# Order changes on VectorE and ScalarE in a two-layer hybrid attention trunk

## The reference

```python
for i in range(DEPTH):                       # DEPTH = 2
    x = x + 0.5 * swiglu(rmsnorm(x, ln_ffn1[i]), w_ffn1_gu[i], w_ffn1_down[i])
    h = rmsnorm(x, ln_mix[i])
    x = x + (even_mixer(h, ...) if i % 2 == 0 else odd_mixer(h, ...))
    x = x + 0.5 * swiglu(rmsnorm(x, ln_ffn2[i]), w_ffn2_gu[i], w_ffn2_down[i])
    gate = jax.nn.sigmoid(rmsnorm(x, ln_ple[i]) @ w_ple_gate[i])
    x = x + gate * (p[i] @ w_ple_proj[i])
return rmsnorm(x, ln_final)
# rmsnorm(x, g) = x * rsqrt(mean(x * x) + 1e-6) * g;  swiglu = (silu(x Wg) * (x Wu)) Wd
```

## Time and profile before

| | |
|---|---|
| median of 3 runs | 1047.08 us (1047.06 to 1048.47) |
| the profiled execution's own time | 1047.2 us |
| its span, first to last instruction | 1045.5 us |
| TensorE (PE) matmuls | busy 1030.4 us, 99% of the span, 6596 instructions |
| TensorE weight loads (PEld) | busy 921.8 us, 88% |
| VectorE (DVE) | busy 757.4 us, 72% |
| ScalarE (ACT) | busy 587.9 us, 56% |
| GpSimd (POOL) | busy 51.6 us, 5% |
| mean granted TensorE clock | 0.997 of full speed |
| device memory read | 183.59 MB, 177 GB/s over the span |
| chain that ended last | PE 94%, DVE 4%, issue 1%, ACT 1%, DMA 1% |

### The profile page before, as it was taken

How to read it: one execution, slowest core, us unless ns; L and a number is a source line. 1 busy time by engine, 2 the same in 40 slices (tenths; PEclk the granted TensorE clock), 3 DMA queues, 4 the chain that set the end, 5 groups by cost and what they waited for, 6 DMA issues and landing times.

```text
span 1045.5 us, 18268 instructions
## 1 busy us (share of the span) xinstructions
PE 1030.4 (99%) x6596; PEld 921.8 (88%) x6596; DVE 757.4 (72%) x1352; ACT 587.9 (56%) x1003; POOL 51.6 (5%) x100
## 2 busy tenths in 40 slices
PE   9999999999999999999999999999999999999996
PEld 8888888998888888888998888889987888888896
DVE  5988765667658887765888787656766787886576
ACT  6666545545646665554666565445654665654463
POOL 1000001000011000000010000010000200000000
PEclk9999999999999999999999999999999999999998
DMA  9675457594315655457647654577733376545741
GB/s 318 211 234 165 143 160 212 175 299 135 116 63 189 214 171 183 132 166 231 215 143 238 196 173 139 155 208 223 241 112 102 126 239 194 189 138 147 212 148 41
DMA packets 225384, 185.52 MB, mean 177 GB/s; under 512 B 3665, under 2 KB 223537, under 8 KB 225201
## 3 DMA queue, kind: packets, MB, share of 16 engines
q1 hardware_dynamic: 222832, 180.94, 55.5%
q10 hardware_dynamic: 2496, 3.86, 1.1%
HBM read 183.59 MB, written 1.07 MB: 177 GB/s over the span
## 4 chain that ended last, share of the span: by engine, by line
PE 94%; DVE 4%; issue 1%; ACT 1%; DMA 1%; DVEq 0%; SPq 0%; ACTq 0%
PE ps L1386 42%; PE ps L1391 22%; PE ps L1317 4%; PE ps L1308 4%; PE ps L1309 4%; PE ps L1310 4%; PE ps L1318 2%; PE ps L1501 2%; PE ps L1502 2%; PE ps L1503 2%; DVE wsp L895 1%; PE ps L1577 1%; PE ps L1590 1%; PE ps L1618 1%; DVE probs L1110 1%
## 5 line engine op out<-in xcount | busy, mean ns | idle before, releaser
L895 DVE TENSOR_TENSOR wsp<-raw,wsp 128x1024 fp32r<-128x1024 f32 (+1 forms) x381 | 416.3, 1109 | 59.9 <-ACT wsp L590 59.1
L590 ACT ACTIVATE wsp<-raw 128x1024 fp32r<-128x1024 f32 (+1 forms) x381 | 354.4, 957 | 25.5 <-PE ps L1310 20.6
L1386 PE MATMUL ps<-xsA,wsp 128*128 128x512 f32 x960 | 229.0, 391 | 0.0
L1386 PEld LDWEIGHTS ps<-xsA,wsp 128*128 128x128 f32 x960 | 176.4, 188 | 34.3
L1386 PE MATMUL ps<-hff,wsp 128*128 128x512 f32 x616 | 145.0, 390 | 0.0
L1386 PEld LDWEIGHTS ps<-hff,wsp 128*128 128x128 f32 x616 | 113.8, 188 | 22.8
L1391 PEld LDWEIGHTS ps<-xsA,wsp 128*128 128x128 f32 x960 | 122.9, 191 | 4.5
L1391 PE MATMUL ps<-xsA,wsp 128*128 128x256 f32 x960 | 124.7, 283 | 0.0
L910 DVE TENSOR_TENSOR sq<-ps,sq 128x512 f32<-128x512 f32 x88 | 60.5, 688 | 87.4 <-ACT sq L606 87.0
L606 ACT ACTIVATE sq<-ps 128x512 f32<-128x512 f32 x88 | 51.9, 590 | 110.7 <-PE ps L1391 109.0
L652 ACT ACTIVATE xsA<-xT,gains 128x256 fp32r<-128x256 f32 x48 | 24.4, 507 | 135.2 <-DVE xT L1044 120.4
(11 more groups left out here) (205 smaller groups left out, 1440.5 us busy)
## 6 DMA issues: line engine op xcount, KB each, us to landing
raw<-in_w_ffn_gu_dram SPq DMA_DIRECT2D x87, 1024.0 KB, 5.1
raw<-in_w_ffn_down_dram SPq DMA_DIRECT2D x64, 704.0 KB, 4.6
raw<-in_w_in_even_dram SPq DMA_DIRECT2D x11, 1024.0 KB, 6.2
raw<-in_w_in_odd_dram SPq DMA_DIRECT2D x9, 1024.0 KB, 6.1
raw<-in_w_ple_gate_dram SPq DMA_DIRECT2D x8, 1024.0 KB, 5.8
raw<-in_w_out_even_dram SPq DMA_DIRECT2D x4, 1024.0 KB, 5.1
raw<-in_w_out_odd_dram SPq DMA_DIRECT2D x4, 1024.0 KB, 7.0
raw<-in_w_ple_proj_dram SPq DMA_DIRECT2D x2, 1024.0 KB, 4.9
```

The source lines that it names most:

```text
L590: act.activation(wsp[:, s, 0, half * n:(half + 1) * n], raw[:, s, half * n:(half + 1) * n], ACT.Copy).then_inc(hi, 1)
L895: dve.tensor_tensor(wsp[:, s, 1, sl], raw[:, s, sl], wsp[:, s, 0, sl].bitcast(F32), ALU.subtract).then_inc(lo, 1)
L1386: pe.matmul(ps[:, bank, :], whi, moving.rearrange("p s t -> p (s t)"), start=first and i == 0, stop=False)
```

## The change

Four places are edited.

1. `mixer_in` on VectorE calls `inverse_root` with `ahead=2`: two units go between the diagonals and the wait for `row_done`.
2. In an even attention step of a softmax group, VectorE divides head i before the units, not behind them.
3. In the last token group, the squares of the last two column groups are summed by VectorE (`add_squares`: a product with a running sum, whose start is the sum so far) and no longer by ScalarE. The sum of the first two and the epsilon are folded in ahead (`squares_so_far`). The last inverse root is the square root from ScalarE's table, its reciprocal on VectorE and one Newton turn (`last_root`), in place of the bit trick and three turns. ScalarE loads the table for the square root behind its last sigmoid. The first token group is done as before.
4. In `first_tiles`, TensorE computes the second chunk in runs: eight high products of tile 2, eight of tile 3, each four of them behind their half's `hi`, and then the low products of both.

```diff
@@ ScalarE, ple_rows
-                    if i:
+                    if 1 <= i < 7:
                         squared(i - 1)
                     advance(ptr[0] + 2)
                     if i == 5:
                         scaled(0)
-                squared(len(GATE_ROWS) - 1)
+                nc.scalar.preload_act_table_set("sqrt_and_others")
+                act.wait_ge(var_ready, 1)
+                act.activation(rfin[:, 1:2], var[:, 1:2], ACT.Sqrt).then_inc(root_taken, 1)
                 scaled(1)
@@ VectorE, mixer_in
-                        inverse_root(norm)
+                        inverse_root(norm, ahead=2)
@@ VectorE, attention_step
                     logits(g + 1)
+                    normalise(g)
                     advance(units)
-                    normalise(g)
@@ VectorE, ple_rows
+                def squares_so_far():
+                    part = rtmp[:, 1:2]
+                    dve.wait_ge(row_squared, 6)
+                    step(dve.tensor_scalar(part, row_sq[:, 4:5], row_sq[:, 5:6], 1.0 / D_MODEL, ALU.add, ALU.mult))
+                    dve.tensor_scalar(part, part, EPS, None, ALU.add).then_inc(part_ready, 1)
+
+                def add_squares(i, start, total, done):
+                    dve.tensor_tensor_reduce(sq[:, i % 2], yT[:, i], yT[:, i], 1.0 / D_MODEL, start, ALU.mult, ALU.add, total).then_inc(done, 1)
+
+                def last_root():
+                    v, y, tmp, half = var[:, 1:2], rfin[:, 1:2], rtmp[:, 0:1], nhalf[:, 1:2]
+                    dve.wait_ge(var_ready, 1)
+                    dve.tensor_scalar(half, v, -0.5, None, ALU.mult).then_inc(nstep, 1)
+                    state["n"] += 1
+                    dve.wait_ge(root_taken, 1)
+                    step(dve.reciprocal(y, y))
+                    step(dve.tensor_scalar(tmp, y, y, half, ALU.mult, ALU.mult))
+                    dve.tensor_scalar(y, tmp, 1.5, y, ALU.add, ALU.mult).then_inc(rfin_ready, 1)
+                    dve.wait_ge(rfin_ready, 2)
@@ VectorE, ple_rows, in the loop over the row tiles
+                    if i == 6:
+                        squares_so_far()
+                        dve.wait_ge(part_ready, 1)
+                        dve.wait_ge(row_squared, 6)
+                        add_squares(6, rtmp[:, 1:2], rcol[:, 0:1], part_ready)
+                    if i == 7:
+                        dve.wait_ge(part_ready, 2)
+                        add_squares(7, rcol[:, 0:1], var[:, 1:2], var_ready)
                     advance(ptr[0] + 2)
...
-                final_root(1)
+                last_root()
@@ TensorE, first_tiles
-                for r in range(1, RING):
+                tiles = [[(chunk_w(1, k, n * P), xs[:, k]) for k in range(KD)] for n in range(2)]
+                for n in range(2):
+                    reuse(2 + n)
+                    for b in range(2):
+                        pe.wait_ge(hi, 3 + b)
+                        high_run(2 + n, tiles[n][4 * b:4 * b + 4], first=b == 0)
+                for n in range(2):
+                    for b in range(2):
+                        pe.wait_ge(lo, 3 + b)
+                        mm = low_run(2 + n, tiles[n][4 * b:4 * b + 4], last=b == 1)
+                    mm.then_inc(tile_done, 1)
+                for r in range(2, RING):
```

More of the change, by code:

```diff
@@ L293, in trunk @@
         row_squared, row_scaled, rfin_ready = sem("row_squared"), sem("row_scaled"), sem("rfin_ready")
+        part_ready, var_ready, root_taken = sem("part_ready"), sem("var_ready"), sem("root_taken")
         y_low, y_high, stored = sem("y_low"), sem("y_high"), sem("stored")
```

## The result

| | before | after |
|---|---|---|
| median, first comparison | 1047.07 us (4 runs, 1046.94 to 1048.47) | 1041.39 us (4 runs, 1041.16 to 1041.61) |
| ratio | | 0.9941, 95% interval 0.9928 to 0.9953 |
| median, second comparison | 1047.41 us (9 runs) | 1041.71 us (5 runs); 0.9943, 0.993 to 0.9957 |
| profiled execution, its span | 1047.2 us, 1045.5 us | 1041.61 us, 1039.9 us |
| VectorE, ScalarE busy | 757.4, 587.9 us | 757.4, 588.3 us |

What follows compares the result with a forecast made beforehand. TensorE's work, its few stops and the end were taken to bound the kernel. Terms 1.35 + 2.0 + 1.4 + 0.2 = 4.95 us off the profiled 1047.2 gave 1042.1 us against the median, range 1041.0 to 1044.2.

Steps and rivals of the forecast that it cites:

- What bounds the kernel: Whole kernel: PE is busy 99% of the span, so time is TensorE's work, its few stops and the end.
- Part 1: Mixer input, both layers: two units ahead remove TensorE's stops of 0.61 and 0.54 us before tile 4; gain 1.35 us.
- Part 2: Even softmax steps: dividing ahead of the unit removes five TensorE stops, 2.1 us, less 0.15 at the long stop; 2.0 us.
- the long stop: Layer 1, 790.25 us, head 10: VectorE is full, so the stop moves to head 12's transposes; -0.15 us.
- Part 3: Kernel end, last `yT` to first scaling: shorter squares and root, table load hidden behind the last sigmoid; gain 1.4 us.
- the two unseen operations: Kernel end: running-sum product taken as 0.48 us and ScalarE's root as 0.22, both from nearest rows.
- Part 4: Second chunk at the start: computing in runs takes 5.57 us instead of 5.79; gain 0.2 us, bounds 0 and 0.25.
- A: Kernel end: the table switch isn't hidden, Part 3 gives 0.35 us, total 1043.2 us; chance 10%.
- B: Softmax steps: Part 2 is given back everywhere and gives 0, total 1044.1 us; chance 10%.
- C: Layer 1: the long stop shortens for good, head 12's logits coming earlier, 0.94 + 0.15 more, 1041.0 us; chance 7%.
- D: Seven softmax steps: units arrive late, TensorE stops 1.1 us in each, total 1051.9 us, slower; chance 3%.
- E: All parts: the change does less than it says, half swallowed by other waits, total 1044.6 us; chance 7%.

Runs made afterwards that it cites:

- e7: The changed kernel with ScalarE's square-root table loaded only once the variance is ready, behind a one-column copy: 1043.28 us, 1.57 more than the changed kernel.
- e6: The changed kernel with layer 1's mixer output taking its two VectorE units behind the division of head 12: 1040.70 us, against 1041.71 for the changed kernel.
- e11: The kernel before, unchanged, profiled again to find where slow runs lose time: 1048.62 us.
- e15: The kernel before plus an unused load of the square-root table on ScalarE after the last squares: ratio 0.9997 to the kernel before.
- e16: The kernel before with three semaphores declared and used by nothing: ratio 1.0003 to the kernel before.
- e1: The kernel before with only two units put ahead in the row wait of both mixers: 1045.86 us, ratio 0.9986.

## Where the prediction held, and which steps failed

**What bounds the kernel** held: the time is TensorE's work, its stops and the tail, and stops read from starts, not brackets, gave each of parts 1 to 3 to 0.15 us.

**Part 1**, 1.35 forecast, 1.40 measured. **Part 2**, 2.0 forecast, 2.13: the five removed stops gave 2.25 for 2.1, and the long stop moved on to head 12, 0.98 and 1.35 us for the "about 1 us" and "about 1.4", at a cost of 0.12 for 0.15. **Part 3**, 1.4 forecast, 1.48: of the two unseen operations the product with the running sum is shown 0.48 long and the root started 0.53 us after it (forecast 0.58), and the root took 0.20; the load was hidden with 0.25 us to spare, 0.2 forecast. (Its lower bound, for operations of 1.0 and 0.4 us, comes out at 0.7 and not at 0.6.) **Part 4**, 0.2 forecast and 0.22 between the two traces, was right by luck: see below. Sum 4.95 forecast, 5.23 by the same terms in the traces.

The rivals: A (the switch not hidden) fell, in the trace and by e7; B (given back everywhere) fell, layers 0 and 1 kept 1.17 and 1.08 us; C (the long stop shortens) didn't come by itself, but e6 shows the 1.2 us were to be had; D (units late) fell, no stop appeared in any softmax step; E fell, the parts add up.

**What failed** is the range. The four runs have their median at 1041.39 us, inside it, but the ratio 0.9941 on the 1047.08 of before is 1040.9, just under the low end of 1041.0; the second comparison's 0.9943 would give 1041.1. The gain was larger than the sum of 4.95 us: 5.7 by the medians, 6.2 by the first ratio. Two steps fell short. The first is in part 2: the long stop was counted at its length alone, 1.9 us before and 0.98 + 1.35 after, "-0.15 us here". It has a second price, the fall of the clock behind it, 1.18 us in about three runs of ten, some 0.35 us in the mean; part 2 removes that too. The 1048.47 among the runs shown may have been of this kind. The second is part 4's term together with the start. The prediction took the 5.79 us of the second chunk for what the old order of products costs, and 5.57 for the new one. The old order takes 5.54 to 5.60 where nothing is late; the 0.22 was a short wait for VectorE's low part and its restart. That wait is longer in six of the nine other traces with the old order (0.13 to 0.38 us) and absent in three, so "Bounds 0 and 0.25" was too narrow: part 4 gives 0 to 0.5 us. The start up to the third chunk became 0.52 to 0.68 us earlier in the traces, where the sum had 0.2. Some 0.4 of this goes with part 3 by the medians, and its cause stays open. Below the sum the range had room for rival C alone.

## What to carry to other kernels

Take the stops between products from their starts and add them up; here this gave three of four parts to 0.15 us, and what remains between the sum and the medians is a finding: sort the runs by their granted clock before averaging, and read the start in more than one trace, since a wait may show there only in some. Before a difference between two orders of work is called the price of the order, look for an execution in which the old order waits for nothing. A stop of nearly 2 us on TensorE can cost more than its length, so splitting it in two helps even where the sum of the two is longer. Where the filler work of a loop stands ahead of what the bottleneck waits for, first turn the order, and where the engine is full, move the filler on to the first stretch in which the engine idles.

## What the runs showed of the hardware

- Behind a stop of 1.9 us TensorE ran at a granted clock of 0.50 for 3.4 us in the three traces of the upper group (e11, e15, e16), from 0.9 to 1.6 us after it had resumed; the eight other traces with that stop don't show it. 44 of 146 executions with that stop are of this group by their mean clock, and none of 34 whose stops are at most 1.35 us.
- At the start TensorE's small products start 0.21 us apart, and later 0.11. A trace's first record of the clock, at full speed, begins at about that time: at 5.21 us in the trace of before, at 6.94 in that of the changed kernel, from 4.53 to 6.94 in 17 of the 18 traces, and at 11.17 in e1's. What lies ahead of the first record is counted as 1.00 in the clock column and in the mean clock, so neither shows this. In e1's trace the first product came at 11.24 us instead of 9.37:

```profile
6.91 1.97 PE L1758 MATMUL ps<-ident,xin 128*128 128x128 f32 x8 [0.15 <-DMA xin<-in_x_dram]
9.52 1.85 PE L1758 MATMUL ps<-ident,xin 128*128 128x128 f32 x8
```

  The same eight products took 1.09 us in the trace of before. e1's 1047.43 us, 1.6 over its usual and at a mean clock of 0.998, are this.
- A switch of ScalarE's table costs 1.30 us from the load's start to the next activation when nothing hides it (e7).
- VectorE's product of two 128x256 tiles in its own memory with a running sum is shown 0.48 us long, and the reading of its sum, 0.08 long, starts 0.41 us after it.
